# Attention halves turned at the end of their slot, values in the middle of the next; first maximum ahead of the combination; even dense pieces

## Chip, cores and metric

One Trainium2 chip (trn2), one of its cores. The metric is the device time of one execution in microseconds (us), the median of several runs.

## The reference

The kernel computes a two-layer encoder trunk on x (1, 1024, 1024), all in float32. Each layer projects a normed input to queries, keys and values of three groups of attention heads, adds one output projection of their outputs, and then a squared-ReLU MLP. Cut to what matters:

```python
for l in range(DEPTH):                                  # 2
    proj = rmsnorm(x, g_mix[l]) @ w_in[l]
    # A: 4 heads, differential: softmax(q1 k1) - lam * softmax(q2 k2), times v (128 wide), then rmsnorm per head
    # B: 4 heads, window of the last 2 chunks of 64 keys, with a sink logit in maximum and sum
    # C: 4 heads, causal with forget gates: s + cum[q] - cum[k]
    x = x + concat([o_a, o_b, o_c]) @ w_out[l]
    x = x + square(relu(rmsnorm(x, g_mlp[l]) @ w_up[l])) @ w_down[l]
return rmsnorm(x, g_final)
# inside each group, for a block of 128 queries:
s = q @ k.T * scale + bias          # only allowed keys
p = softmax(s)                      # A: a = p[0] - lam * p[1]
o = p @ v
```

## The kernel before

Every float32 product is made of three matmuls of a faster type: each operand is split into a high part (rounded, a copy by ScalarE) and a low part (the rest, a subtraction by VectorE), and high*high, low*high and high*low are summed in PSUM. So everything that TensorE multiplies must first pass through ScalarE and then VectorE.

The part that the change touches is the attention loop, one per layer. Its work is a list of 64 *steps*: eight pairs of heads in the order B0, B1, C0, C1, A0, A1, A2, A3, and in each pair i = 0 to 7, the blocks of 128 queries. A step covers `window(t)` blocks of keys: at most 2 in B, i + 1 in C and A. Scores of up to 512 keys are one *phase*; steps with more than 4 key blocks have two (`phases(t)`), and both use the same PSUM tile ps[0], so that the second scores wait until the first are read.

What a step t goes through:
- TensorE makes the scores (`scores`, L1211).
- VectorE adds the bias, takes the maximum of each row and writes to probs (`biased_max`, L888, once per phase), then the negated maximum (L900 for B, L904 for two phases, L907 else).
- ScalarE takes exponentials in place (`exponentials`, L613; the sink's at L616), j = 0 and 1 for the two score maps of the pair.
- In A pairs VectorE then combines both maps into one (`combine`, L920); in B and C it inverts the sums (`invert_sums`).
- One step later TensorE turns (transposes) the result in *halves* of up to four 128x128 blocks into one of two banks of ps[2] (`turn_half`, L1264); ScalarE takes the high part (`half_high`, L631), VectorE the low part (`half_low`, L943).
- TensorE multiplies a half with V into ps[3] (`values`, L1284 and L1286), VectorE adds up both columns (`sum_values`, L952 and L961), and ScalarE scales the output or squares it for the later norm (`finish_o`, L646 and L639).

A *slot* is the unit of the order written out by hand: each half of step t-1 gets one slot in step t, so a step has one to four slots (A: one half per four key blocks; C: the same for each of two heads). In the slots of steps 56, 57, 58 and 62 halves of finished head outputs are turned too, for the output projection (mix slots, L626 and L938). The engines all run over the same list of slots, each in its own fixed order, and meet through semaphores.

Between these, to fill TensorE, stand *pieces* of the projection for later pairs: a slab of 128 output columns is 8 pieces (one per 128 input rows) of six matmuls of 512 columns (`piece`, L1116), accumulated in ps[1] alone, so the next slab's first piece waits until VectorE has taken the slab out (`evacuate`, L801 for Q and L804 for K and V). Then ScalarE and VectorE split it (`part_high` L576, `part_low` L814, L816); a V slab is turned first (L1097, then L571 and L811). `PIECES` says how many pieces each step of a pair gets. Weights come by DMA into one buffer w_raw, are split by ScalarE (w_hi, L520) and GpSimd (w_lo, L498), from slab 23 on by VectorE (w_lo, L769), and only then is the next load issued on SP's queue. From slab 23 the slabs belong to the output projection (`add_out`, L979); xw_hi (L514) is a further load there.

TensorE's order in a slot before:

```python
early = (len(s.pieces) + 1) // 2
if s.first and t < NT:
    scores(t, 0)
dense(s.pieces[:early])
if s.half: turn_half(s.half)
if s.values: values(s.values)        # the half of the slot before
...                                  # a V slab is turned here
if s.first and t < NT and phases(t) == 2:
    scores(t, 1)
dense(s.pieces[early:])
```

## Time and profile before

| what | us |
|---|---|
| median of 3 runs (2870.1 to 2870.88) | 2870.24 |
| the profiled execution | 2878.04 |
| its span, first to last instruction | 2876.2 |
| TensorE busy (93% of the span) | 2674.1 |
| VectorE busy | 1164.2 |
| ScalarE busy | 897.7 |
| GpSimd busy | 192.8 |
| mean granted TensorE clock | 0.952 of full speed |

The durations come from the one profiled execution. TensorE is busy nearly all of the time, but a busy figure also counts time at a lower granted clock. The kernel has stages with different limits: the attention loops lie at about 87 to 645 us (layer 0) and 1497 to 2058 us (layer 1), with a tail of some 20 us each, and between and behind them come output projection and MLP. A row of the view by windows reads: stretch (us from the span's start), its length, busy us of TensorE's matmuls, its weight loads, VectorE, ScalarE and GpSimd (each with its count), then the mean granted clock of TensorE, the DMA share and GB/s.

### The profile page before, as it was taken

What the parts mean: (1) busy time and instruction counts of PE and PEld (TensorE: products, weight loads), DVE (VectorE), ACT (ScalarE), POOL (GpSimd) and SP (SyncE); (2) the same over time, 40 slices, a digit from 0 to 9 for tenths busy, and PEclk for the clock granted to TensorE, in tenths of its full rate; (3) what the DMA queues carried; (4) which work ended last, traced back from release to release, by engine and by line L of the source; (5) the groups of instructions that cost most, each with busy time, mean ns of one, the idle gap of its engine ahead of it and who ended that gap; (6) DMA issues with size and microseconds to landing.
All of it is one profiled execution on the core that took longest, in us unless ns stands there. A gap on an engine that the chain in (4) does not pass through costs nothing.

```text
span 2876.2 us, 34048 instructions
## 1 busy us (share of the span) xinstructions
PE 2674.1 (93%) x12857; PEld 2175.5 (76%) x12857; DVE 1164.2 (40%) x2367; ACT 897.7 (31%) x1580; POOL 192.8 (7%) x91
## 2 busy tenths in 40 slices
PE   8989988778999999999999989887799999999998
PEld 6777766657888888888877777665688888888886
DVE  5553455555322322223336445555553222232233
ACT  5543333443221212112236343343332112121222
POOL 1010111001000000000210110110020000000001
PEclk9998899988999999999999989997899999999999
DMA  5000000021111111111210000001111111111112
GB/s 165 23 23 15 23 23 23 21 64 47 37 51 51 44 51 46 49 51 51 95 44 23 23 15 23 23 23 53 35 52 44 51 44 51 44 51 51 44 51 73
DMA packets 218717, 127.22 MB, mean 44 GB/s; under 512 B 15182, under 2 KB 214392, under 8 KB 218616
## 3 DMA queue, kind: packets, MB, share of 16 engines
q1 hardware_dynamic: 213192, 114.35, 13.9%
q10 hardware_dynamic: 5424, 11.54, 1.1%
q8 instruction: 62, 1.02, 0.2%
q14 instruction: 39, 0.32, 0.0%
HBM read 113.27 MB, written 12.58 MB: 44 GB/s over the span
## 4 chain that ended last, share of the span: by engine, by line
PE 84%; DVE 7%; ACT 5%; issue 3%; DMA 1%; DVEq 0%; SPq 0%; ACTq 0%; POOL 0%; POOLq 0%
PE ps L1116 72%; PE ps L1264 3%; PE ps L1211 3%; PE ps L1284 2%; ACT probs L613 2%; PE ps L1286 1%; DVE probs L920 1%; ACT pt_hi L631 1%; PE ps L1097 1%; DVE part L804 1%; PE ps L1161 1%; DVE part L801 1%; DVE probs L888 1%; DVE pt_lo L943 1%; DVE wide_lo L938 0%
## 5 line engine op out<-in xcount | busy, mean ns | idle before, releaser
L1116 PE MATMUL ps<-wide_hi,w_hi 128*128 128x512 f32 x3016 | 976.8, 406 | 66.2 <-DVE part L804 31.9
L1116 PE MATMUL ps<-wide_lo,w_hi 128*128 128x512 f32 x3016 | 947.9, 396 | 0.0
L1116 PE MATMUL ps<-wide_hi,w_lo 128*128 128x512 f32 x3016 | 944.8, 395 | 0.0
L1116 PEld LDWEIGHTS ps<-wide_hi,w_hi 128*128 128x128 f32 x3016 | 555.5, 192 | 203.8 <-issue 90.0
L1116 PEld LDWEIGHTS ps<-wide_lo,w_hi 128*128 128x128 f32 x3016 | 578.7, 192 | 125.9
L1116 PEld LDWEIGHTS ps<-wide_hi,w_lo 128*128 128x128 f32 x3016 | 576.1, 191 | 124.3
L631 ACT ACTIVATE pt_hi<-ps 128x512 fp32r<-128x512 f32 (+3 forms) x216 | 110.0, 511 | 482.0 <-PE ps L1264 481.9
L687 ACT ACTIVATE w_hi<-w_raw 128x1024 fp32r<-128x1024 f32 x112 | 117.8, 1051 | 451.8 <-PE ps L1116 450.7
L943 DVE TENSOR_TENSOR pt_lo<-ps,pt_hi 128x512 fp32r<-128x512 f32 (+3 forms) x216 | 126.5, 587 | 301.1 <-ACT pt_hi L631 301.1
L1284 PE MATMUL ps<-v_parts,pt_hi 128*128 128x128 f32 (+1 forms) x696 | 204.5, 353 | 21.9 <-DVE pt_lo L943 21.9
L691 ACT ACTIVATE ring<-ring 128x1024 f32<-128x1024 f32 x64 | 67.8, 1060 | 492.2 <-DVE ring L1051 492.2
L1071 DVE TENSOR_TENSOR xt<-ps,xt 128x1024 f32 x48 | 58.8, 1225 | 387.5 <-PE ps L1116 387.5
L1051 DVE SCALAR_TENSOR_TENSOR ring<-ps,inv_rms 128x1024 f32<-128x1024 f32 x64 | 78.4, 1225 | 331.4 <-PE ps L1116 314.6
L613 ACT ACTIVATE probs<-probs,neg_max,slope 128x256 f32<-128x256 f32 (+7 forms) x256 | 201.3, 788 | 14.2 <-DVE neg_max L904 10.3
L1264 PE MATMUL ps<-ident,probs 128*128 128x128 f32 x696 | 130.0, 305 | 73.0 <-DVE probs L920 73.0
L1264 PEld LDWEIGHTS ps<-ident,probs 128*128 128x128 f32 x696 | 95.1, 157 | 105.2 <-issue 86.6
L1284 PEld LDWEIGHTS ps<-v_parts,pt_hi 128*128 128x128 f32 x696 | 150.5, 216 | 30.0 <-DVE pt_lo L943 27.6
L1286 PE MATMUL ps<-v_parts,pt_lo 128*128 128x64 f32 (+1 forms) x696 | 170.8, 253 | 0.0
L498 POOL TENSOR_TENSOR w_lo<-w_raw,w_hi 128x1024 fp32r<-128x1024 f32 x42 | 104.2, 2481 | 903.2 <-ACT w_hi L520 903.2
L1286 PEld LDWEIGHTS ps<-v_parts,pt_lo 128*128 128x128 f32 x696 | 150.9, 217 | 0.1
L1054 DVE TENSOR_TENSOR wide_lo<-ring,wide_hi 128x1024 f32 x64 | 78.4, 1226 | 158.1 <-ACT wide_hi L693 158.1
L1047 DVE TENSOR_TENSOR w_lo<-w_raw,w_hi 128x1024 fp32r<-128x1024 f32 x112 | 136.4, 1218 | 0.4 <-ACT w_hi L687 0.4
(140 smaller groups left out, 1899.8 us busy)
## 6 DMA issues: line engine op xcount, KB each, us to landing
w_raw<-in_w_up_dram SPq DMA_DIRECT2D x128, 256.0 KB, 3.0
w_raw<-in_w_down_dram SPq DMA_DIRECT2D x128, 256.0 KB, 3.0
w_raw<-in_w_in_dram SPq DMA_DIRECT2D x92, 256.0 KB, 3.3
x_saved<-xt ACTq DMA_DIRECT2D x16, 512.0 KB, 2.6
w_raw<-in_w_out_dram SPq DMA_DIRECT2D x32, 256.0 KB, 3.3
xt<-x_saved SPq DMA_DIRECT2D x16, 512.0 KB, 3.6
out_dram<-rows SPq DMA_DIRECT2D x4, 1024.0 KB, 6.7
first_rows<-in_x_dram ACTq DMA_DIRECT2D x3, 1024.0 KB, 13.3
```

The costliest lines, as they stand in the source:

```text
L498: nc.gpsimd.tensor_tensor(w_lo[:, j], w_raw[:], w_hi[:, j].bitcast(F32), ALU.subtract).then_inc(w_split, 1)
L613: e = A.activation(probs[:, (2 * t + j) % 4, 0:width], probs[:, (2 * t + j) % 4, 0:width], ACT.Exp, bias=neg_max[:, at:at + 1], scale=sl, ...
L631: A.activation(pt_hi[:, bank, 0:half.blocks], src.rearrange("p (b q) -> p b q", q=P), ACT.Copy).then_inc(pt_hi_done, 1)
L687: A.activation(w_hi[:, w_slot(l, FFN_DONE + j)], w_raw[:], ACT.Copy).then_inc(w_hi_done, 1)
L943: V.tensor_tensor(pt_lo[:, bank, 0:half.blocks], src.rearrange("p (b q) -> p b q", q=P), pt_hi[:, bank, 0:half.blocks].bitcast(F32), ALU.s ...
L1047: V.tensor_tensor(w_lo[:, z], w_raw[:], w_hi[:, z].bitcast(F32), ALU.subtract).then_inc(w_split, 1)
L1051: V.scalar_tensor_tensor(out=ring[j][:], in0=ps[j][:], scalar=0.0, in1=inv_rms[:], op0=ALU.max, op1=ALU.mult).then_inc(evacuated, 1)
L1116: mm = T.matmul(ps[p][:, bass.ts(t, BANK)], w, h[:, bass.ts(t, BANK)], start=(start and n == 0), stop=(stop and n == 2))
L1211: mm = T.matmul(ps[0][:, BANK * j:BANK * j + key1 - key0], q[half, q_slot(p), i * P:(i + 1) * P], k[half, kv_slot(p), k0 * P + key0:k0 * P ...
L1264: tr = T.transpose(ps[2][:, at:at + P], src[:, b * P:(b + 1) * P], ident[:])
L1284: T.matmul(o.rearrange("p (h e) -> p h e", h=2), pt_hi[:, bank, at], v_parts[:, kv_slot(p), k0 + b, :, e], start=(b == 0), stop=False)
L1286: mm = T.matmul(o[:, 0:w], pt_lo[:, bank, at], v_parts[:, kv_slot(p), k0 + b, 0, e], start=False, stop=(b == blocks - 1))
```

## The change

On TensorE, the half of a slot is turned at the slot's end, and the values of the slot before stand behind its early pieces, ahead of the second scores; the turn of a V slab moves up to just behind the first scores. On VectorE, the first maximum of a step comes ahead of the combination (or inversion) of the step before, and the low part of a half behind the evacuation. On ScalarE, a slot's exponentials come ahead of its high part, the first exponentials of a two-phase step in its first slot instead of its second; `finish_o` comes one slot later. The maximum of the second phase starts from that of the first, so that one negation serves both. `PIECES` is more even, and of a slot's pieces at least two, or all but one, count as early. From pair 2 on the first slot of i = 0 gets no piece.

```diff
--- before.py
+++ after.py
@@ -37,6 +37,7 @@
         self.pieces, self.ends, self.ended, self.split = [], None, None, []
         self.turns_v = None
         self.summed = None
+        self.stored = None
         self.exps = []
 
 
@@ -119,9 +120,9 @@
     PHASE0 = [sum(phases(u) for u in range(t)) for t in range(NT + 1)]
     NPHASE = PHASE0[NT]
 
-    PIECES = {0: [2] * 8, 1: [2] * 8, 2: [0, 3, 4, 4, 4, 4, 3, 2], 3: [0, 3, 4, 4, 4, 4, 3, 2]}
+    PIECES = {0: [2] * 8, 1: [2] * 8, 2: [0, 3, 3, 3, 3, 4, 4, 4], 3: [3, 3, 3, 3, 3, 3, 3, 3]}
     for p in range(FIRST_A, PAIRS - 1):
-        PIECES[p] = [0, 4, 4, 4, 3, 3, 3, 3]
+        PIECES[p] = [2, 3, 3, 3, 3, 3, 3, 4]
     PIECES[PAIRS - 1] = [0, 1, 3, 4, 4, 3, 3, 0]
     MIX_AT = {56: [0, 1], 57: [2, 3], 58: [4, 5], 62: [6]}
     SCALE_AT = {FIRST_A * NQ + 2 * NQ + 3: (0, 2), FIRST_A * NQ + 3 * NQ + 3: (2, 3)}
@@ -174,6 +175,8 @@
             now = [s for s in mine if s.step % NQ == i]
             want = PIECES[p][i] + held
             for k, s in enumerate(now):
+                if i == 0 and k == 0 and p >= 2:
+                    continue
                 n = -(-want // (len(now) - k))
                 for _ in range(n):
                     if not todo:
@@ -192,6 +195,7 @@
         s.values = last.half if last and last.half and last.half.slab is None else None
         if s.values and s.values.last:
             s.summed = s.values.step
+        s.stored = last.summed if last else None
         done = slots[n - 1].ends if n else None
         if done is not None and (done >= IN or SLABS[done][1] != V_):
             s.ended = done
@@ -207,7 +211,7 @@
     for t in range(NT):
         now = [s for s in slots if s.step == t]
         for j in range(2):
-            at = 0 if phases(t) == 1 else 1 + j
+            at = 0 if phases(t) == 1 else j
             now[min(at, len(now) - 1)].exps.append(j)
 
     def load_done(n):
@@ -651,19 +655,21 @@
                     A.activation(o_inv[:, n0 * NQ:n1 * NQ], o_inv[:, n0 * NQ:n1 * NQ], ACT.Sqrt).then_inc(o_rms, 1)
 
                 for s in slots:
-                    if s.half:
-                        half_high(s.half)
                     if s.ended is not None and s.ended < IN:
                         part_high(s.ended)
                     for j in s.exps:
                         exponentials(s.step, j)
-                    if s.summed is not None:
-                        finish_o(s.summed)
+                    if s.stored is not None:
+                        finish_o(s.stored)
+                    if s.half:
+                        half_high(s.half)
                     for n in s.split:
                         split_load(l, n)
                     if s.step in SCALE_AT and s.first:
                         rms_of_heads(*SCALE_AT[s.step])
 
+                if slots[-1].summed is not None:
+                    finish_o(slots[-1].summed)
                 finish_o(NT - 1)
                 rms_of_heads(3, 4)
                 split_load(l, EXTRA + 1)
@@ -876,6 +882,8 @@
                     if before:
                         dve.wait_ge(turned, NHALF * l + before[-1])
                     V.memset(wait_slot[:], 0.0)
+                    if ph:
+                        dve.wait_ge(scores_read, NPHASE * l + PHASE0[t] + 1)
                     to = far_max if ph else row_max
                     a = (2 * t) % 8
                     for j in range(2):
@@ -887,8 +895,8 @@
                             bias = o_out[:, FIRST_A + 2 * n + j, key0:key1]
                         e = V.tensor_tensor_reduce(out=probs[:, (2 * t + j) % 4, key0:key1],
                                                    in0=ps[0][:, BANK * j:BANK * j + key1 - key0], in1=bias, scale=1.0,
-                                                   scalar=-3e38, op0=ALU.add, op1=ALU.max,
-                                                   accum_out=to[:, a + j:a + j + 1])
+                                                   scalar=row_max[:, a + j:a + j + 1] if ph else -3e38,
+                                                   op0=ALU.add, op1=ALU.max, accum_out=to[:, a + j:a + j + 1])
                     e.then_inc(scores_read, 1)
                     if key1 < width:
                         return
@@ -899,12 +907,8 @@
                             at = 4 * l + 2 * p + j
                             e = V.tensor_scalar(neg_max[:, a + j:a + j + 1], row_max[:, a + j:a + j + 1], sink[:, at:at + 1],
                                                 neg_slope[:, 2 * p + j:2 * p + j + 1], ALU.max, ALU.mult)
-                    elif ph:
-                        for j in range(2):
-                            e = V.tensor_scalar(neg_max[:, a + j:a + j + 1], row_max[:, a + j:a + j + 1],
-                                                far_max[:, a + j:a + j + 1], neg, ALU.max, ALU.mult)
                     else:
-                        e = V.tensor_scalar(neg_max[:, a:a + 2], row_max[:, a:a + 2], neg, None, ALU.mult)
+                        e = V.tensor_scalar(neg_max[:, a:a + 2], to[:, a:a + 2], neg, None, ALU.mult)
                     e.then_inc(max_done, 1)
 
                 def combine(t):
@@ -982,19 +986,15 @@
                 dve.wait_ge(cum_out, CH * (l + 1))
                 for s in slots:
                     t = s.step
+                    if s.first and t < NT:
+                        biased_max(t, 0)
                     if s.first and t:
                         if ORDER[(t - 1) // NQ][0] == "A":
                             combine(t - 1)
-                    if s.first and t < NT:
-                        biased_max(t, 0)
-                    if s.half:
-                        half_low(s.half)
+                        else:
+                            invert_sums(t - 1)
                     if s.first and t < NT and phases(t) == 2:
                         biased_max(t, 1)
-                    if s.first and t and ORDER[(t - 1) // NQ][0] != "A":
-                        invert_sums(t - 1)
-                    if s.summed is not None:
-                        sum_values(s.summed)
                     if s.ended is not None and s.ended < IN:
                         part_low(s.ended)
                     if s.ends is not None:
@@ -1002,6 +1002,10 @@
                             evacuate(s.ends)
                         else:
                             add_out(s.ends - OUT)
+                    if s.half:
+                        half_low(s.half)
+                    if s.summed is not None:
+                        sum_values(s.summed)
                     for n in s.split:
                         if n >= IN:
                             split_load(l, n)
@@ -1290,20 +1294,20 @@
 
                 for s in slots:
                     t = s.step
-                    early = (len(s.pieces) + 1) // 2
+                    early = max(min(2, len(s.pieces)), len(s.pieces) - 1)
                     if s.first and t < NT:
                         scores(t, 0)
-                    dense(s.pieces[:early])
-                    if s.half:
-                        turn_half(s.half)
-                    if s.values:
-                        values(s.values)
                     if s.turns_v is not None:
                         pe.wait_ge(evacuated, EVACS * l + slab_of(s.turns_v, V_) + 1)
                         turn(part, ps[1], NQ, v_turned)
+                    dense(s.pieces[:early])
+                    if s.values:
+                        values(s.values)
                     if s.first and t < NT and phases(t) == 2:
                         scores(t, 1)
                     dense(s.pieces[early:])
+                    if s.half:
+                        turn_half(s.half)
 
                 def out_piece(k, slab, p, start, stop):
                     j = w_slot(l, OUT + k)
```

## Rows read from the trace of the kernel before

**Rows 1.** The page, its 40 slices: TensorE busy in tenths.
```profile
PE   8989988778999999999999989887799999999998
```

**Rows 2.** TensorE's waits over the span: us in total, times, longest us.
```profile
PE ps L1264 <- DVE probs L920: 73.0, 36, 5.9
...
PE ps L1116 <- DVE part L804: 31.9, 12, 3.0
...
PE ps L1284 <- DVE pt_lo L943: 21.9, 21, 2.9
```

**Rows 3.** Windows: B, C0, C1, A0, A1, A2, A3 of layer 1; A1 of layer 0.
```profile
1496.80:1575.60 78.80, 76.03 (x450) 59.91 (x450) 46.83 (x177) 49.09 (x144) 7.16 (x3) 0.97 0.08 22
1575.60:1658.70 83.10, 74.26 (x425) 60.15 (x424) 37.05 (x114) 33.84 (x77) 7.25 (x3) 0.91 0.07 20
1658.70:1748.30 89.60, 80.73 (x457) 66.79 (x456) 38.52 (x116) 33.68 (x77) 7.23 (x3) 0.89 0.07 18
1748.30:1822.00 73.70, 65.61 (x358) 51.91 (x356) 40.55 (x122) 26.98 (x66) 7.61 (x3) 0.93 0.08 22
1822.00:1895.10 73.10, 63.19 (x334) 49.87 (x332) 41.55 (x123) 28.03 (x67) 7.68 (x3) 0.91 0.09 23
1895.10:1972.90 77.80, 64.21 (x336) 49.83 (x334) 44.71 (x127) 30.85 (x70) 8.55 (x4) 0.91 0.08 21
1972.90:2076.00 103.10, 74.37 (x375) 59.17 (x375) 59.07 (x149) 42.71 (x90) 1.90 (x1) 0.81 0.19 55
413.70:484.00 70.30, 59.81 (x336) 46.53 (x334) 41.67 (x123) 28.10 (x67) 7.65 (x3) 0.98 0.09 23
```

**Rows 4.** VectorE's groups by shape: busy us, mean ns of one, idle before.
```profile
L943 DVE TENSOR_TENSOR pt_lo<-ps,pt_hi 128x512 fp32r<-128x512 f32 x128 | 88.2, 691 | 152.9 <-ACT pt_hi L631 152.8
...
L804 DVE TENSOR_TENSOR part<-ps,inv_rms 128x1024 f32<-128x1024 f32 x28 | 34.1, 1218 | 21.3 <-PE ps L1116 21.1
...
L904 DVE TENSOR_SCALAR neg_max<-row_max,far_max,neg_slope 128x1 f32<-128x1 f32 x96 | 21.8, 269 | 5.3 <-issue 0.9
...
L888 DVE CUSTOM_DVE_ANT_0 probs<-ps,near 128x256 f32<-128x256 f32 x56 | 21.4, 420 | 14.6 <-issue 14.6
...
L888 DVE CUSTOM_DVE_ANT_0 probs<-ps,far 128x384 f32<-128x384 f32 x32 | 16.5, 553 | 10.6 <-issue 10.6
...
L907 DVE TENSOR_SCALAR neg_max<-row_max,neg_slope 128x2 f32<-128x2 f32 x48 | 12.5, 260 | 5.0 <-issue 0.4
...
L920 DVE SCALAR_TENSOR_TENSOR probs<-probs,lam_ratio 128x1024 f32<-128x1024 f32 x8 | 10.3, 1285 | 0.6
```

**Rows 5.** TensorE's timeline in layer 0, pair A1 and A2's start.
```profile
456.27 0.30 PE L1264 MATMUL ps<-ident,probs 128*128 128x128 f32 x1 [0.79 <-DVE probs L920]
...
461.30 0.47 PE L1116 MATMUL ps<-wide_hi,w_hi 128*128 128x512 f32 x1 [2.98 <-DVE part L804]
...
462.76 0.27 PE L1264 MATMUL ps<-ident,probs 128*128 128x128 f32 x1
...
469.97 0.73 PE L1116 MATMUL ps<-wide_hi,w_hi 128*128 128x512 f32 x2
...
472.83 0.38 PE L1264 MATMUL ps<-ident,probs 128*128 128x128 f32 x2
...
488.19 0.45 PE L1264 MATMUL ps<-ident,probs 128*128 128x128 f32 x1 [3.67 <-DVE probs L920]
```

**Rows 6.** ScalarE's groups by shape, columns as in the groups above.
```profile
L631 ACT ACTIVATE pt_hi<-ps 128x512 fp32r<-128x512 f32 x128 | 75.7, 594 | 260.2 <-PE ps L1264 260.2
...
L613 ACT ACTIVATE probs<-probs,neg_max,slope 128x256 f32<-128x256 f32 x80 | 47.2, 591 | 1.4 <-DVE neg_max L907 1.2 <-DVE neg_max L900 0.2
...
L646 ACT ACTIVATE o_out<-o_out,inv_sum 128x64 f32<-128x64 f32 x128 | 37.1, 338 | 48.5 <-DVE o_out L961 48.5
...
L613 ACT ACTIVATE probs<-probs,neg_max,slope 128x896 f32<-128x896 f32 x24 | 27.0, 1126 | 0.0
...
L616 ACT ACTIVATE sink_exp<-sink,neg_max,slope 128x1 f32<-128x1 f32 x64 | 23.9, 374 | 0.0
```

## The prediction

> **What bounds the kernel now.** I read the page first. TensorE's tenths show where it is slack: slices 2 to 9 and 21 to 29 [rows 1]. These are the two attention loops (one per layer), and everything that the diff touches lies in them. Next, TensorE's waits [rows 2]: longest for the combination (L920), then for a projection slab to be taken out of PSUM (L804, and L801 for Q slabs), then for low parts (L943). Then the loop of layer 1 pair by pair [rows 3]. Stretch less TensorE's busy time is its idle time: B pairs 2.8, C0 8.8, C1 8.9, A0 8.1, A1 9.9, A2 13.6, A3 with the tail 28.7 us, in all 81 us a layer. VectorE and ScalarE are busy at most 62% of any stretch, so it is the order of the work that costs time, not its amount.
>
> The half-rate clock is the second loss. Pair A1 took 70.3 us in layer 0 at a mean clock of 0.98 and 73.1 us in layer 1 at 0.91 [rows 3]. The 0.07 are 10 us more at 1.2 GHz instead of 2.4, and they cost 2.8 us: 0.28 us for each us at half rate. Over the 579 us from B to A3 the mean clock is about 0.91, so some 105 us at half rate, 29 us lost a layer.
>
> **The change, part by part.** No engine gets work worth counting, and no DMA is added; SP's loads wait for w_split as before. Removed: in the 24 two-phase steps of a layer (i = 4 to 7 of the C and A pairs) two L904 instructions become one of L907's form, 269+269 to 260 ns [rows 4]: 0.25 us off a dependent chain. Added: row_max as scalar operand of the second maximum, and a wait on VectorE's own first maximum. No row shows the operand; nearest is L904, which reads such a column and takes 9 ns more than L907, which reads none. From below nothing, from above 0.1 us a step (the wait on itself with it), 5 us in all; I take 0, as the first maximum ended long before.
>
> Moved at no price of its own: finish_o a slot later (nobody waits for it before the mix slots), the turn of V to behind the first scores (what then waits is in the terms "V slab" below), and the same 24 pieces a pair spread more evenly, where they fall being part of each walk.
>
> *Combination and turn later.* Before, in step i=5 of A1, TensorE does scores and one piece and then waits 0.79 us at the turn for the combination; the slab that ended there costs 2.98 us more; in step i=0 it has no piece at all and waits 3.7 us [rows 5]. Now the turn stands at the slot's end, behind its pieces, values and second scores.
>
> *What comes in its place.* ScalarE's order in a slot is now exponentials, then high part. In the first slot of a two-phase step the exponentials need the second maximum, and this the second scores, which TensorE issues just ahead of the turn. So the high part of that half is queued behind second maximum, negation and first exponentials; after it comes the low part; and TensorE wants both after one piece of the next slot. For A, i=6, from the end of the second scores: 0.05 + two maxima of 384 (0.55+0.48) + 0.1 + negation 0.23 + 0.03 + exponentials of 896 1.03 (1126 ns, less the 0.1 by which neighbours overlap) + high part 0.59 + 0.03 + low part 0.69 + 0.14 = 3.9 us [rows 4, 6]. Cover: turn 0.38 and one piece 1.46 (461.30 to the next engine work at 462.76) [rows 5], 1.84. Wait: 2.1 us. In the same way i=7 of A (two pieces cover) 1.2; and C, i = 4, 5, 6, 7: 1.35, 1.7, 2.1, 2.5, together 7.65 a pair.
>
> *Slots without a piece.* There values follow directly on their own turn: high 0.59 + low 0.69 + hops 0.2 = 1.5 us uncovered [rows 4, 6]. The plan leaves such slots last in C1's i = 5, 6, 7 and in A0's i=0: four times 1.5 a layer. Before, the transposes of the next half stood between.
>
> *Pair by pair, TensorE's idle us a layer* (before from [rows 3]):
> - C0: V slab at i=1 0.5, slab at i=3 0.3, and 7.65: 8.45; before 8.8: **-0.4**.
> - C1: V slab at i=0 1.4, slab at i=5 0.2, 7.65, three bare slots 4.5: 13.75; before 8.9: **+4.9**.
> - A0: V slab 1.4, bare slot 1.5, i=5 2.65, i=6 2.1, i=7 1.2: 8.85; before 8.1: **+0.8**. The i=5, from its start: VectorE begins the first maximum at 2.85, behind the low part of i=4, ends it at 4.2 and the combination at 5.65; TensorE is ready for the turn at 5.15 and, with the hop, waits 0.65. The second maximum ends at 6.85, the slab's evacuation (1.22) [rows 4] at 8.1; its next piece was wanted at 6.2: 2.0.
> - A1: i=0 2.85, i=3 0.2, then as A0: 9.0; before 9.9: **-0.9**. The i=0: low part of i=7's last half at 1.1, first maximum to 2.0, combination of 1024 (1.29 and two small ones) [rows 4] to 3.9; TensorE is ready at 2.0; then the V slab's low part ends 0.85 later than the turn.
> - A2: the same, and 1.4 for the w_lo that VectorE makes itself in i=5: 10.4; before 13.6: **-3.2**.
> - A3: walked the same way. The first piece of slab 25 waits 2.85 for w_lo (before 1.6), since VectorE comes to it after the half of i=3, whose high part is behind both exponentials. The second exponentials of i=5 still stand behind xw_hi, which waits for its DMA: this was the longest wait, 5.9 [rows 2], and is now spread over a low part (4.0), second scores (1.1) and the turn (0.9). Second scores ahead of the turn in i=7 give time back. From slab 24 to the tail +0.4, mix slots of i = 0, 1 -0.4: **0**.
>
> *Fewer switches.* Two pieces in one run take 2.86 us (469.97 to 472.83), one alone 1.46 [rows 5] and up to 0.1 more after scores: 0.06 to 0.2 saved where two runs become one. Four merges in each of three A pairs, at 0.13: **-1.5**.
>
> *B pairs.* The slab waits go (-2.8), and 16 merges at 0.2, since both runs there follow another kind of work, take 3.2: a full step of 4.67 us, from 4.88. But VectorE and ScalarE now form a ring: maxima and negation 1.33 (two of 0.42, two of 0.27, less overlap), exponentials with sinks 1.82 (0.59 and 0.37, twice, overlapped), scaling of the outputs 0.5 (0.34 twice, overlapped), high part 0.6, low part 0.65, value sum 0.25: 5.15 us [rows 4, 6]. That is longer than the step. The slack is used up after five steps or so; ten more cost 0.48 each and two short ones give 1 back: +3.8. B: **-2.2**.
>
> Sum a layer: -2.2 -0.4 +4.9 +0.8 -0.9 -3.2 +0 -1.5 = -2.5; two layers -5.
>
> *The clock.* The long waits shrink: before, some twelve of 2.8 us or more a layer; now about three, but fifteen of 2.0 to 2.6. Half rate follows such waits: the transpose behind 3.67 us takes 0.45 us where the one behind 0.79 takes 0.30 [rows 5]. Bounds: nothing comes back, or all of 29 us a layer. I take 2 a layer, near nothing, since as many waits remain as go: -4. The Trainium skill (TensorE: Matmul & The Clock Gate, "HAM oscillation") says that waits between bursts of matmuls throttle the engine when they are long, and that short ones leave it at full rate. By that rule alone the sum would be that of rival 2.
>
> Total -9: the profiled execution's 2878.04 us would be 2869. It lies 7.8 above the median of the timed runs, 2870.24, so the median becomes **2861**. A tie is anything within 0.2% (5.7 us), about what a measurement of this kernel can tell from no change.
>
> **Rivals.**
> 1. *The ring of VectorE and ScalarE decides: slower.* For A, i=7, it is first maximum 1.5, combination 1.9, second maximum and negation 1.7, exponentials 1.3, high part 0.6, exponentials 1.4, high and low part and sum 1.7: 10.1 us, as long as TensorE's step of four pieces (9.7). If lag carried over makes each of the 48 two-phase steps 0.5 us longer than I sum, it is +24: 2885. It decides from 0.2 us each. For it: no reserve in i = 5 to 7. Against: VectorE is busy only 57% of A1 [rows 3].
> 2. *The clock recovers.* Waits of 2.6 us keep full rate; of the 58 us two thirds come back, less a third of that for the waits that stay: -26 where I take -4: 2838. For it: 10 us less at half rate were worth 2.8 in A1. Against: waits of 2 to 3 us every ten.
> 3. *The late turn hides nearly everything.* The waits for L920 (73.0) go and nothing replaces them: about 2800. Against: the order on ScalarE above.
> 4. *No net effect.* One wait for another, 2870.
>
> **How the numbers follow.** Forecast (own range 2850 to 2871) 0.36, of it 0.26 beyond the tie and 0.10 in it; rival 1 0.32 (0.28 slower, 0.04 tie); rival 2 0.14; rival 3 0.06; rival 4 0.12 (0.08 tie, 0.04 slower). Faster 0.46, same 0.22, slower 0.32. The range, 2828 to 2893, holds the forecast, rivals 2 and 4 and most of rival 1, with the 5 us of the unpriced operand; it leaves out rival 3.
>
> **What would show it.** Waits for L920 and for the slabs fall to a third or less; those for L943 grow from 21.9 to 80 or more, some 2 us each, at i = 4 to 7 of C and A; the B stretch is 76 to 77 us, C1 longer than 92; busy times of VectorE and ScalarE stay. I am wrong if the low-part waits stay small (then rival 3), if B steps stay at 4.7, or if steps i = 5 to 7 of the A pairs exceed 12 us (rival 1).

## The result, and the profile after

The changed kernel takes **2885.65 us** (median of 4 runs, 2882.95 to 2887.71), the one before 2870.17 beside it: ratio 1.0056, 95% interval 1.0038 to 1.0073. So it is 15 us slower, where the forecast was 9 us faster. The number lies in the range given, and the sign was wrong. Its profiled execution took 2882.95 us (span 2881.1, mean clock 0.954), that of before 2878.04. The two profiles alone show only a third of the loss, so a second one of each kernel was taken; what follows uses both.

TensorE's waits of the kernel after (us in total, times, longest us); they answer to [rows 2]. L947 is the low part (L943 before), L924 the combination (L920), L810 the evacuation of K and V slabs (L804):
```profile
PE ps L1288 <- DVE pt_lo L947: 88.1, 54, 3.2
PE ps L1268 <- DVE probs L924: 17.5, 22, 1.7
PE ps L1120 <- DVE part L810: 16.9, 10, 2.3
```
The combination went from 73.0 to 17.5, slabs from 31.9 to 16.9, and low parts from 21.9 to 88.1, 1.6 us each. This is the exchange that the prediction describes.

Windows of layer 1 (B, C0, C1, A0, A1, A2, A3 with the tail; length, PE busy, ... granted clock as third from the end), as in [rows 3]:
```profile
1498.50:1575.50 77.00, 75.28 (x450) 61.48 (x450) 45.11 (x174) 46.28 (x135) 7.12 (x3) 0.98 0.10 28
1575.50:1659.60 84.10, 73.93 (x423) 58.40 (x422) 39.20 (x114) 35.79 (x83) 7.17 (x3) 0.94 0.07 20
1659.60:1756.30 96.70, 82.70 (x459) 66.45 (x458) 37.77 (x112) 35.11 (x76) 7.10 (x3) 0.89 0.07 17
1756.30:1833.10 76.80, 69.45 (x359) 54.61 (x358) 43.00 (x118) 29.77 (x68) 7.16 (x3) 0.88 0.08 21
1833.10:1900.50 67.40, 59.82 (x333) 46.45 (x332) 41.17 (x118) 28.11 (x66) 7.20 (x3) 0.97 0.09 24
1900.50:1973.40 72.90, 62.93 (x335) 48.90 (x334) 44.06 (x123) 31.00 (x69) 9.11 (x4) 0.93 0.08 23
1973.40:2080.45 107.05, 78.42 (x375) 59.63 (x375) 55.79 (x143) 40.48 (x86) 1.90 (x1) 0.76 0.18 53
```
Length less busy time is idle time. In C1 it is 14.0 us (13.75 forecast, 8.9 before), in A2 10.0 (10.4 forecast, 13.6 before). In A3 with the tail it is 28.6, as before (28.7), but TensorE's busy time there rose from 74.4 to 78.4 us at a clock of 0.76 instead of 0.81 [rows 3]. So the case is decided by busy time too, and not by the waits alone.

The same stretch, C1, in three places: layer 0 of the first profile of the changed kernel,
```profile
250.60:345.00 94.40, 80.40 (x457) 64.67 (x456) 37.84 (x112) 35.01 (x76) 7.10 (x3) 0.91 0.07 18
```
and layers 0 and 1 of its second profile:
```profile
255.80:356.40 100.60, 86.61 (x457) 69.53 (x456) 37.77 (x112) 35.10 (x76) 7.10 (x3) 0.84 0.06 16
...
1672.70:1767.20 94.50, 80.51 (x459) 64.76 (x458) 37.85 (x112) 34.98 (x76) 7.09 (x3) 0.91 0.06 17
```
The idle time is 14.0 us in all three. What varies is how much of the work runs at 1.2 GHz. From 0.91 of 94.4 us to 0.84 of 100.6 us are 15 us more at half rate (twice 0.16 of 100.6, less twice 0.09 of 94.4), and they cost 6.2: 0.41 us each, not the 0.28 that the prediction took.

Over both loops with their tails, from the first scores to the first piece behind the last step, the sums are:

| | idle us | busy us |
|---|---|---|
| before, two profiles | 160.9, 160.1 | 994.8, 992.6 |
| after, two profiles | 164.8, 164.8 | 1001.6, 1010.8 |
| difference of the means | +4.3 | +12.5 |

Together 16.8 us, of which the rest of the program gives 4.6 back in these four executions; the loss is 15.5 us here and, by its ratio, some 21 in the repeat below.

The 12.5 us of busy time have two parts. One is the clock: over both loops and tails (twice the length of a window times what its clock lacks of 1) TensorE was granted 1.2 GHz for 225 and 225 us before, and for 226 and 250 after. At 0.41 us each these 13 us more are some 5, an estimate. The other part is there at an unchanged clock. The first profile of the changed kernel has as much time at half rate as the kernel before, and yet 7 to 9 us more busy time. The loop of layer 1, before and after:
```profile
1496.80:2057.54 560.74, 487.77 (x2672) 388.77 (x2673) 296.37 (x899) 237.97 (x570) 47.37 (x20) 0.91 0.09 26
...
1498.49:2059.15 560.66, 491.11 (x2671) 387.10 (x2672) 295.88 (x876) 240.69 (x571) 46.75 (x20) 0.91 0.10 27
```
The executions say the same: at a mean clock of 0.953 the kernel before took 2866.9 to 2872.3 us (11 executions), the changed one 2884.9 to 2887.7 (3). So of the 16.8 us some 4 are waiting, 5 the lower clock, and 7 busy time that the new order costs at the same clock. That half rate fell on dearer work does not explain them: with each matmul put at the mean that it has at the full clock between the same neighbours, over all profiles here, the loops come to 903 and 902 us before and 910 and 911 after (high_first of experiment 1: 906, hf_bare of experiment 7: 903), an estimate. No run isolates these 7. What the traces show is that TensorE is interrupted more often: in the loops it idled for longer than 0.15 us 102 and 98 times before, and 126 and 125 times after (100 in high_first, 88 in hf_bare). And a run is dearer at its start: in the timeline at the end of this section the first matmul of the values takes 0.39 us behind its wait, the next of its kind (478.06) 0.33.

How one late low part comes about, in the timeline of layer 0, pair A1, step i=6, second slot (start, duration, in brackets the wait before):
```profile
473.68 0.63 PE L1268 MATMUL ps<-ident,probs 128*128 128x128 f32 x4
...
475.02 0.23 DVE L911 TENSOR_SCALAR neg_max<-far_max,neg_slope 128x2 f32<-128x2 f32 x1
475.29 1.14 ACT L617 ACTIVATE probs<-probs,neg_max,slope 128x896 f32<-128x896 f32 x1 [5.04 <-DVE neg_max L911]
...
476.42 0.57 ACT L635 ACTIVATE pt_hi<-ps 128x512 fp32r<-128x512 f32 x1
...
477.03 0.69 DVE L947 TENSOR_TENSOR pt_lo<-ps,pt_hi 128x512 fp32r<-128x512 f32 x1 [1.78 <-ACT pt_hi L635]
...
477.77 0.39 PE L1288 MATMUL ps<-v_parts,pt_hi 128*128 128x256 f32 x1 [2.08 <-DVE pt_lo L947]
```
The half is turned by 474.31. ScalarE had been idle for 5 us, but in its order the exponentials come first, and they wait for the negation; the high part starts 2.1 us after it could have. The values wait 2.08 us; the prediction says 2.1.

### The profile page after: what moved, and what is told of

Its sections match the earlier page's. It is cut to its first block, busy times and chain, and to the rows that moved or that the text cites. A ratio compares the mean times of both kernels' runs of the same rounds, so it can differ in the third digit from the quotient of the medians.

```text
span 2881.1 us, 34000 instructions
## 1 busy us (share of the span) xinstructions
PE 2675.7 (93%) x12857; PEld 2168.9 (75%) x12857; DVE 1161.7 (40%) x2319; ACT 901.9 (31%) x1580; POOL 191.6 (7%) x91
## 3 DMA queue, kind: packets, MB, share of 16 engines
q8 instruction: 62, 1.02, 0.1%
## 4 chain that ended last, share of the span: by engine, by line
PE 73%; issue 10%; DVE 9%; ACT 6%; DVEq 2%; DMA 0%; SPq 0%; ACTq 0%; POOL 0%; POOLq 0%
PE ps L1120 64%; PE ps L1288 3%; DVE probs L896 2%; PE ps L1268 2%; ACT pt_hi L635 2%; DVE pt_lo L947 1%; ACT probs L617 1%; PE ps L1290 1%; PE ps L1215 1%; DVEq L903 1%; DVE neg_max L911 1%; PE ps L1165 1%; DVEq L920 1%; ACT wide_hi L630 1%; DVE probs L924 0%
## 5 line engine op out<-in xcount | busy, mean ns | idle before, releaser
L1120 PE MATMUL ps<-wide_hi,w_hi 128*128 128x512 f32 x3016 | 977.4, 406 | 44.1 <-DVE part L810 16.9
L947 DVE TENSOR_TENSOR pt_lo<-ps,pt_hi 128x512 fp32r<-128x512 f32 (+3 forms) x216 | 127.0, 588 | 378.9 <-ACT pt_hi L635 378.7
L1288 PE MATMUL ps<-v_parts,pt_hi 128*128 128x128 f32 (+1 forms) x696 | 186.7, 328 | 88.6 <-DVE pt_lo L947 88.1
L1288 PEld LDWEIGHTS ps<-v_parts,pt_hi 128*128 128x128 f32 x696 | 144.6, 208 | 122.9 <-DVE pt_lo L947 116.4
L1055 DVE SCALAR_TENSOR_TENSOR ring<-ps,inv_rms 128x1024 f32<-128x1024 f32 x64 | 78.4, 1225 | 329.9 <-PE ps L1120 313.1
L1268 PE MATMUL ps<-ident,probs 128*128 128x128 f32 x696 | 131.0, 305 | 17.7 <-DVE probs L924 17.5
L1058 DVE TENSOR_TENSOR wide_lo<-ring,wide_hi 128x1024 f32 x64 | 78.4, 1226 | 158.1 <-ACT wide_hi L699 158.1
L1268 PEld LDWEIGHTS ps<-ident,probs 128*128 128x128 f32 x696 | 82.6, 151 | 32.7 <-issue 28.5
```

The source lines that it names most:

```text
L947: V.tensor_tensor(pt_lo[:, bank, 0:half.blocks], src.rearrange("p (b q) -> p b q", q=P), pt_hi[:, bank, 0:half.blocks].bitcast(F32), ALU.s ...
L1055: V.scalar_tensor_tensor(out=ring[j][:], in0=ps[j][:], scalar=0.0, in1=inv_rms[:], op0=ALU.max, op1=ALU.mult).then_inc(evacuated, 1)
L1058: V.tensor_tensor(u_lo[:, 2 * m + j], ring[j][:], u_hi[:, 2 * m + j].bitcast(F32), ALU.subtract).then_inc(u_split, 1)
L1120: mm = T.matmul(ps[p][:, bass.ts(t, BANK)], w, h[:, bass.ts(t, BANK)], start=(start and n == 0), stop=(stop and n == 2))
L1268: tr = T.transpose(ps[2][:, at:at + P], src[:, b * P:(b + 1) * P], ident[:])
L1288: T.matmul(o.rearrange("p (h e) -> p h e", h=2), pt_hi[:, bank, at], v_parts[:, kv_slot(p), k0 + b, :, e], start=(b == 0), stop=False)
```

## The experiments

**Repeats.** Each kernel unchanged, for a second profile (above) and a second ratio.

> The kernel before, unchanged, for a second profile. Theory A (the loss lies in the order of the engines) expects 2867 to 2873 us, idle time of TensorE from B to the start of step 63 again 73 us a layer, and time at half rate within 25 us of the first profile. Theory B (the half-rate clock differs from execution to execution enough to make the difference) expects a profiled time that differs by 8 us or more from the first profile's 2878, with the idle time unchanged.

Measured: 2868.09, ratio 0.9996 (0.9977 to 1.0015).

> The changed kernel, unchanged, for a second profile and a second ratio. Theory, the loss is real and the same each time: ratio 1.004 to 1.007, 2880 to 2890. Rival, most of the 15 us was the scatter of executions: ratio 1.000 to 1.003.

Measured: 2893.9, ratio 1.0072 (1.0044 to 1.0100), just above what was expected. The loss is real.

**1. The high part ahead of the exponentials.** ScalarE's order in a slot becomes slab's high part, half's high part, exponentials. finish_o, which now runs closer to its successor on the scratch tile o_junk, gets a wait for its own last squaring:
```diff
+                    if s.half:
+                        half_high(s.half)
                     for j in s.exps:
                         exponentials(s.step, j)
                     if s.stored is not None:
                         finish_o(s.stored)
-                    if s.half:
-                        half_high(s.half)
```


> The changed kernel, but ScalarE takes a half's high part ahead of the exponentials of the same slot (with a wait of each squaring in the A pairs on the one before, since both write the same scratch tile). Theory A (the high part queued behind the exponentials costs about 2 us in each of 48 two-phase steps) expects the waits for low parts to fall from 88 to 30 us or less and the time to 2820 to 2845 us. The rival (VectorE's and ScalarE's chain through the step sets its length, in whatever order) expects the waits to move to the combination and the time to stay within 2875 to 2890.

Measured: **2807.45**, ratio 0.9797 (0.9764 to 0.9831), 78 us faster than the change and 63 faster than before. The same slot as above:
```profile
444.66 0.63 PE L1270 MATMUL ps<-ident,probs 128*128 128x128 f32 x4 [1.24 <-DVE probs L926]
...
445.33 0.60 ACT L635 ACTIVATE pt_hi<-ps 128x512 fp32r<-128x512 f32 x1 [4.08 <-PE ps L1270]
...
445.96 0.69 DVE L949 TENSOR_TENSOR pt_lo<-ps,pt_hi 128x512 fp32r<-128x512 f32 x1
...
446.70 0.39 PE L1290 MATMUL ps<-v_parts,pt_hi 128*128 128x256 f32 x1
```
The high part starts 0.04 us after the turn's end, and the values don't wait; the turn itself waits 1.24 us for the combination (see the last section). Waits for low parts fall to 41.7 us in all, not to the 30 that was expected. Pair C0 in both layers:
```profile
161.50:234.10 72.60, 68.92 (x423) 54.87 (x422) 38.23 (x112) 35.63 (x83) 7.16 (x3) 1.00 0.09 23
...
1533.20:1605.80 72.60, 68.93 (x426) 54.89 (x424) 38.25 (x112) 35.62 (x83) 7.15 (x3) 1.00 0.09 23
```
Idle 3.7 instead of 10.2, busy 68.9 instead of 73.9 to 78.5, at the full 2.4 GHz. Over both loops idle time falls by 40.9 us (to 123.9) and busy time by 41.9 (1006.2 to 964.3): for each us of waiting that went, another of busy time went too. Most of it is clock, with 154 us at half rate in the loops instead of 226 and 250. That is why the gain is beyond what was expected.

**2. Where does the clock come back?** The same edit in the slots of the C pairs only, and everywhere else only:
```diff
+                    early_high = s.half and 2 <= s.step // NQ < FIRST_A
+                    if early_high:
+                        half_high(s.half)
```


> The changed kernel with the high part of a half ahead of the exponentials only in the slots of the two C pairs; elsewhere as in the change. In high_first TensorE's idle time in the C pairs fell from 24.2 to 12.7 us a layer and its busy time there by some 10 us a layer, which is the clock. Theory, idle time and clock go together in the stretch where the wait is, whatever stands elsewhere: 23 us of idle and 15 to 25 of clock come back, 2838 to 2852, and the mean clock of the two C0 stretches is 1.00. Rival, the clock of a stretch follows the whole load, not its own waits: 2855 to 2866, with C0 still at 0.9 to 0.95.

> The complement: the high part first everywhere but in the C pairs. The B pairs' idle time (4.2 and 1.7 us in B1) and that of A0 to A2 (25 to 19 a layer) come back, some 18 us in all, and as much of clock in them. Theory: 2845 to 2860, the C0 stretches stay at 0.88 to 0.94 and C1 at 0.84 to 0.91. Rival, as above: the C stretches' clock rises too and the time is under 2840.

Measured: 2853.29, ratio 0.9941 (0.9925 to 0.9958), and 2849.25, ratio 0.9928 (0.9900 to 0.9956). Pairs C0 and A1 of layer 1 with the C pairs alone,
```profile
1567.10:1640.70 73.60, 69.39 (x424) 54.95 (x424) 37.35 (x115) 35.73 (x83) 7.16 (x3) 1.00 0.09 22
...
1807.80:1875.20 67.40, 59.84 (x335) 46.44 (x334) 41.16 (x118) 28.10 (x66) 7.20 (x3) 0.97 0.09 24
```
and with all but them:
```profile
1562.80:1646.00 83.20, 73.58 (x425) 58.41 (x424) 38.02 (x112) 35.67 (x83) 7.18 (x3) 0.94 0.07 20
...
1815.90:1879.60 63.70, 57.94 (x335) 45.63 (x334) 41.99 (x119) 27.79 (x66) 7.50 (x3) 1.00 0.10 26
```
C0's clock rises with C0's own waits gone, A1's with A1's. The gains over the change are 32.4 and 36.4 us, in sum 68.8 of high_first's 78.2. The theory's place was right, its price for C a little high: idle fell by 25.0 us as expected, busy time by 11 instead of 15 to 25: C1 still has 8.7 us of idle time, and its clock stays at 0.88 to 0.91. The rival, a clock that follows the whole load alone, is out. But a stretch's own waits are not all either: C0 was expected at 1.00 in both layers, and in layer 0 it is 0.96, with the same 4.2 us of idle time as in layer 1. There B1 just ahead of it still has 4.1 us of waits, which high_first, with 1.00 in both, has not.

**3. The rest of ScalarE's new order.** High part first, ahead of the slab's high part too, and the exponentials of two-phase steps a slot later, as before the change:
```diff
-        at = 0 if phases(t) == 1 else j
+        at = 0 if phases(t) == 1 else 1 + j
...
+                    if s.half:
+                        half_high(s.half)
                     if s.ended is not None and s.ended < IN:
                         part_high(s.ended)
...
-                    if s.half:
-                        half_high(s.half)
```


> The changed kernel with ScalarE's order of before in each slot (high part of the half first, then the slab's high part, then exponentials, these one slot later in two-phase steps), finish_o a slot later as in the change. Theory, the change lost its gain by queuing the high part behind the exponentials: 2805 to 2840, waits of the values for the low part below 50 us (88 in the changed kernel). With the exponentials a slot later the combination is later too, so nearer 2830 than high_first's 2807. Rival, the ring of VectorE and ScalarE is too long whatever the order: 2870 to 2890.

Measured: 2876.49, ratio 1.0028 (1.0013 to 1.0043): missed. Low parts fell to 49.6 us as said, but other waits are longer than in high_first (there 28.3, 8.9 and 8.2 for the last three lines in turn):
```profile
PE ps L1290 <- DVE pt_lo L949: 49.6, 38, 3.5
PE ps L1270 <- DVE probs L926: 40.4, 30, 2.9
PE ps L1122 <- DVE v_parts L819: 27.7, 10, 3.0
PE ps L1217 <- DVE row_max L898: 16.7, 13, 3.2
```
From high_first this kernel differs by 69 us, and in two things: the late exponentials, and the half's high part ahead of the slab's. Of the 47.2 us of idle time between them (171.1 and 123.9 in the loops) 18.8 are waits for v_parts. These belong to the second: ScalarE copies a V slab only when it is through with the high part of a half that TensorE turned late. The combination and the first maximum (12.1 and 8.5) fit the late exponentials. So early exponentials look like the good part of the change on ScalarE, and the high part behind them is the bad one (experiment 1); how the 69 us divide was not measured.

This kernel also warns of a simple rule for the clock: it idles 6.3 us more than the change and is busy 26 us less, with some 205 us at half rate.

**4. Single parts of the change on the old kernel.** TensorE's new order alone (with the earlier turn of a V slab and the new count of early pieces, not shown here), and the first maximum ahead of the combination alone:
```diff
-                    if s.half:
-                        turn_half(s.half)
                     if s.values:
                         values(s.values)
...
                     dense(s.pieces[early:])
+                    if s.half:
+                        turn_half(s.half)
```


> The kernel before with only TensorE's order changed: V slab turned behind the first scores, pieces, values, second scores, then the turn at the slot's end. VectorE, ScalarE and the pieces as before. Theory A expects a gain, as high parts are not behind exponentials: waits for the combination from 73 to 35 us or less, for low parts at most 35, 2840 to 2860 us. The rival (a turn late in the slot is itself the loss, since the low part comes late for the values) expects 2875 us or more and waits for low parts above 60 us.

```diff
+                    if s.first and t < NT:
+                        biased_max(t, 0)
                     if s.first and t:
                         if ORDER[(t - 1) // NQ][0] == "A":
                             combine(t - 1)
-                    if s.first and t < NT:
-                        biased_max(t, 0)
```


> The kernel before with only VectorE's order changed: first maximum ahead of the combination. The turn stays in mid slot, so each combination comes 1.4 us later for it. Theory A expects waits for the combination to grow by 1.0 to 1.4 us in 30 to 48 steps, from 73 to 105 to 140 us, and 2900 to 2930 us. A rival (the maximum first frees the exponentials earlier and pays for itself) expects 2870 or less.

Measured: 3070.67, ratio 1.0708 (1.0674 to 1.0743), and 2899.45, ratio 1.0127 (1.0088 to 1.0166). The second came just under what was expected, with 96.5 us of waits for the combination instead of 105 or more. Its idle time in the loops is 23 us above the kernel before, its busy time the same (992.3; before 994.8 and 992.6). The first was missed by 200 us; the rival had the right side, with low parts at 74.7 us and above 2875, but not the size. These waits come with it:
```profile
PE ps L1211 <- DVE row_max L888: 66.7, 29, 5.2
PE ps L1116 <- DVE part L804: 47.9, 12, 4.3
PE ps L1116 <- DVE part L801: 32.4, 14, 2.8
```
VectorE's old order has the low part ahead of the second maximum and of the evacuation. With the turn at the slot's end that low part comes late, and both are queued behind it. The change's TensorE order thus needs its VectorE order; neither part can be priced on the old kernel by itself. (The second kernel of experiment 7 puts the low part alone back ahead of the evacuation, and loses 83 us.)

**5. The pieces.** The change with the old counts:
```diff
-    PIECES = {0: [2] * 8, 1: [2] * 8, 2: [0, 3, 3, 3, 3, 4, 4, 4], 3: [3, 3, 3, 3, 3, 3, 3, 3]}
+    PIECES = {0: [2] * 8, 1: [2] * 8, 2: [0, 3, 4, 4, 4, 4, 3, 2], 3: [0, 3, 4, 4, 4, 4, 3, 2]}
     for p in range(FIRST_A, PAIRS - 1):
-        PIECES[p] = [2, 3, 3, 3, 3, 3, 3, 4]
+        PIECES[p] = [0, 4, 4, 4, 3, 3, 3, 3]
```


> The changed kernel with the piece counts of before (none in step i=0 of C and A pairs). Theory, a slot without a piece leaves a half's values right behind its own turn, 1.5 us uncovered: C1 loses its three such slots, but all slots of i=0 of seven pairs a layer become bare, so 2890 to 2915. Rival, the placing of the pieces doesn't matter because the same work is spread either way: 2880 to 2890. If it is under 2875, the even pieces were a loss by themselves.

Measured: 2954.58, ratio 1.0301 (1.0279 to 1.0322), 69 us more, beyond the expected. Low-part waits go from 54 (88.1 us) to 70 (116.5 us), 28 us, and the span's clock from 0.954 to 0.931. TensorE's idle time over the span rises by 21 us, its busy time by 51 (2675.7 to 2727.0). A slot without a piece is about as dear as expected in waiting, and more than twice that again in busy time.

**6. The maxima.** The change without the operand row_max and its wait, with two negations:
```diff
-                                                   scalar=row_max[:, a + j:a + j + 1] if ph else -3e38,
+                                                   scalar=-3e38,
...
```


> The changed kernel with the maxima of before: second maximum without the operand row_max and its wait, two L904-like negations in place of one. Theory, the shorter chain is worth something: second maximum 0.06 us shorter twice, negations 0.25 longer, so the chain is 0.13 us longer in each of the 48 two-phase steps, 2884 to 2892. Rival, the operand and the added wait on the own semaphore cost more than the negation saves: 2870 to 2882.

Measured: 2889.82, ratio 1.0067 (1.0043 to 1.0091), not to be told from the change's 1.0056 and 1.0072. It is inconclusive on the time. The instruction itself is plain in the groups by shape of the changed kernel:
```profile
L896 DVE CUSTOM_DVE_ANT_0 probs<-ps,far 128x512 f32<-128x512 f32 x80 | 51.9, 686 | 5.5 <-issue 5.5
...
L896 DVE CUSTOM_DVE_ANT_0 probs<-ps,far,row_max 128x512 f32<-128x512 f32 x16 | 11.4, 747 | 10.3 <-issue 10.1
```
The operand costs 61 ns at 512 columns (60 at 384), twice a step: half of the 0.25 us that the single negation saves.

**7. Toward a better version.** high_first, and in a slot without a piece the next turn ahead of the last values (and not at the slot's end again):
```diff
+                    if s.half and not s.pieces:
+                        turn_half(s.half)
                     if s.values:
                         values(s.values)
```


> high_first (2807) with one more edit: in a slot without a piece the turn of the next half is issued ahead of the values of the last one. Theory, in such slots (three in C1, one in A0, some in the B pairs' and the tail's steps) values wait 1.5 us for their own turn, and the tail's +3.1 us a layer comes from this: 2790 to 2801, with the stretch from the scores of step 63 to the first piece behind the last turn back to 33 us or less from 35.8. Rival, the wait only moves (the turn now waits in the same place for the combination or the exponentials): 2803 to 2812.

Measured: **2788.62**, ratio 0.9727 (0.9701 to 0.9753): the fastest kernel here, 97 us below the change. Idle 117.1, busy 958.5. The reason that I gave for the tail was wrong: from the scores of step 63 to the next piece it takes 18.4 and 19.2 us, but high_first already took 18.8 and 19.1, where the change takes 21.3. The gain lies in A0 (73.1 and 72.9 us to 68.9 and 67.9; of it in the first step 15.0 and 15.9 to 13.6) and in A3 (85.2 and 84.5 to 82.8 and 82.0). On top of it, the combination ahead of the first maximum again, and the low part ahead of the evacuation:

> hf_bare (2789) with the combination ahead of the first maximum again, as in the kernel before. It tests that part of the change with the late turn in place. Theory, the first maximum must stand first, since the second scores wait for it and the late turn gives the combination cover: without it the 36 combinations of 1.9 us stand ahead of it, and 0.5 to 1 us of each shows: 2810 to 2830. Rival, the combination is now the last one waited for (39 us at the turn), so giving it precedence pays: 2770 to 2785.

> hf_bare (2789) with the low part of a half ahead of the evacuation of the slab that ends in the same slot, on VectorE. Waits for low parts are 30 us, for evacuations 15. Theory, with the high part early on ScalarE the low part can go as soon as it is there, and slots in which a slab ends lose their wait of 1.2 us: 2778 to 2787. Rival, the low part waits for the high one (4.9 at the longest) and holds the evacuation up behind it, as in the kernel before with the late turn: 2795 to 2830.

Measured: 2808.10, ratio 0.9777 (0.9753 to 0.9801), just under its range, and 2871.93, ratio 1.0009 (0.9994 to 1.0024), above both. So the first maximum ahead of the combination is worth 14 us (by the ratios) to 19 (by the medians) with the late turn, where it costs 1.3% without it (experiment 4). In the second, slabs are waited for again,
```profile
PE ps L1270 <- DVE probs L926: 36.7, 24, 5.3
PE ps L1122 <- DVE part L812: 27.5, 12, 2.7
PE ps L1290 <- DVE pt_lo L949: 27.5, 22, 4.4
PE ps L1122 <- DVE part L809: 24.4, 14, 2.5
PE ps L1103 <- DVE part L812: 19.9, 12, 1.8
```
and the low parts gained 2.6 us (30.1 to 27.5). What waits at the head of VectorE's queue, here a low part whose high part is not there yet, holds what stands behind it.

## Why the prediction was wrong

**The waits were right in sum, in part by luck.** TensorE's idle us a layer, forecast and measured (before: layer 1):

| pair | before | forecast | layer 0 | layer 1 |
|---|---|---|---|---|
| B | 2.8 | 3.8 | 4.2 | 1.7 |
| C0 | 8.8 | 8.45 | 10.1 | 10.2 |
| C1 | 8.9 | 13.75 | 14.0 | 14.0 |
| A0 | 8.1 | 8.85 | 7.8 | 7.4 |
| A1 | 9.9 | 9.0 | 7.6 | 7.6 |
| A2 | 13.6 | 10.4 | 10.0 | 10.0 |
| A3 and tail | 28.7 | 28.7 | 31.7 | 28.6 |

The forecast's idle sum is 83.0 a layer, the measured mean 82.4. (B's forecast is its 2.8, less the slab waits, with the ring's 3.8; its switches are busy time.) C0 missed 1.6 us: its step i=0 has no piece either, a bare slot that my list of four left out, and it measures 1.62 at the price of 1.5 that the list used. A0 and A1 were 1 to 1.5 us too dark, because i=5 measures 1.9 instead of 2.65 and, in A1, i=0 2.15 instead of 2.85. A3 with the tail is 3.0 longer in layer 0, which no step of the walk has. The misses of single pairs, up to 3 us, cancel; the single waits that the theory named (C's 1.5, 1.8, 2.2 and 2.6, and 2.08 in A) are no luck.

**TensorE's busy time was wrong.** It was to fall by 13.4 us (9.4 by *Fewer switches* and the merges of *B pairs*, 4 by *The clock*); it rose by 12.5. Both terms failed, and neither had a case with a loss in it.

*The clock*: long waits go, short ones come, so 4 us come back. Instead some 13 us more were at half rate, about 5 us. Three faults are in it.
- It took half rate to follow the longest waits. In C0 the change idles 1.5, 1.8, 2.2 and 2.6 us in steps i=4 to 7, and the clock is 0.92 and 0.94 (0.88 and 0.92 in the second profile); before it was 0.95 and 0.91, with up to 3.1 us in one step. In high_first 1.5 us are the most in any step of C0, and it is 1.00. Waits of about 2 us thus cost the clock no less than the long ones did.
- It bounded the clock from one side: "nothing comes back" was taken as the worst, so no case of the sum had a loss in it. Yet the change had more waits, if shorter ones.
- It priced half rate at 0.28 us a us, by the length of A1; by busy time the same two rows give 3.4 us for 10, or 0.33, and C1 shows 0.41.

The Trainium skill (TensorE: Matmul & The Clock Gate, "A second HAM failure mode: psum-queue depth-cycling") describes a kernel in which frequent short idle times between groups of matmuls make the clock swing between its levels. C0's 0.88 to 0.94 with 10.2 us of short waits, and 1.00 with 3.7 us of them in high_first, agree with it; the section just ahead of it, which the prediction names beside rival 2, speaks of long waits only, and by it alone the clock should have risen.

*Fewer switches* was mis-sized by more. At an unchanged clock busy time was to fall by 9.4 us and rose by about 7. A full B step was to fall from 4.88 to 4.67 us; it takes 4.82 to 4.84. At a full clock 16 merges give 0.04 each and not 0.2, so some 5 us of the 9.4 were not there. The rest lies in the other pairs, where the sum has twelve merges a layer in the A pairs saving 0.13 each, and nothing for the runs that the new, shorter waits cut. That the cutting is what costs the 7 us is likely from the counts above (some 25 interruptions more, and fewer again in the faster kernels), but not shown.

**The rivals.** Rival 1 gave 2885, which is the number measured, but not for its reason, so that the range held the result is luck: of the steps that were priced one by one, in C0 to A2, none idles 0.5 us longer than forecast, so there is no lag that adds up; B1 alone shows some in layer 0 (4.2 us). Steps i=5 to 7 of the A pairs do pass 12 us now and then, which I had named as its mark. A step of A1, i=7, with 1.08 and 1.10 us of idle took 12.02 and 12.62 us, and in high_first 9.69 with none: the mark was the clock's. Rival 2, a clock that recovers, is seen in another kernel: with most waits for low parts gone, 42 us of busy time come back, most of it clock. Rival 3's 2800 needed exactly what experiments 1 and 7 did.

**What would show it** was met by the waits for low parts and combination (88.1, 1.6 us each, and 17.5), by the B stretch of layer 1 (77.0; layer 0 took 80.0), by C1 above 92 and by the unchanged busy times of VectorE and ScalarE. It was not met by the slabs: their waits fell to a half (K, V and Q together 47.2 to 21.6), not to a third.

What stays open: what exactly the 7 us at an unchanged clock are, why the same stretch gets 0.91 in one execution and 0.84 in another with the same waits, and where in a step the clock falls.

## What to carry to other kernels

When an instruction is moved earlier in an in-order queue, list what now stands behind it and whether it waits for a later event: here the place of one call on ScalarE was the difference between 15 us lost and 63 won. When a transfer of waits is even, busy time decides it, so give it a case with a loss. Where the high part was moved, each us of waiting removed took 0.4 to 1 us of busy time with it (25.0 and 11, 19.9 and 18.7, 40.9 and 41.9 us). That is no law: old_scalar idles 6 us more than the change and is busy 26 less, and before_max_first idles 23 more than the kernel before and is busy as long. Parts of a reordering that only work together can't be priced one at a time on the old kernel, but can be undone one at a time on the new.

## What the runs showed of the hardware

A VectorE instruction of 0.228 us took 2.29 when it was issued beside one of GpSimd. Pair A0's first step, in the changed kernel:
```profile
346.63 2.36 POOL L502 TENSOR_TENSOR w_lo<-w_raw,w_hi 128x1024 fp32r<-128x1024 f32 x1 [38.12 <-ACT w_hi L524]
...
346.72 2.29 DVE L911 TENSOR_SCALAR neg_max<-row_max,neg_slope 128x2 f32<-128x2 f32 x1
```
It ends 0.02 us after GpSimd's. In the first C0 step that has pieces the same negation takes 1.58 us (173.60 to 175.18), to the end of a GpSimd split (172.78 to 175.16). Not every instruction is held: in the same stretch the maximum of 256 columns, which reads its scores from PSUM, takes its usual 0.42 us (173.07). The Trainium skill (SBUF — State Buffer, "SBUF: two separate sides") says that VectorE, in an instruction of a two-port mode or with two inputs in SBUF, shares a pair of ports with GpSimd, and that whichever starts first has the pair until it ends; these rows agree. The combination is held too. That of 768 columns takes 1.02 us on average before, and in high_first, where half of the eight run beside a split, 2.04:
```profile
L920 DVE SCALAR_TENSOR_TENSOR probs<-probs,lam_ratio 128x768 f32<-128x768 f32 x8 | 8.1, 1019 | 0.6
...
L926 DVE SCALAR_TENSOR_TENSOR probs<-probs,lam_ratio 128x768 f32<-128x768 f32 x8 | 16.3, 2038 | 0.6
```
In the slot shown in experiment 1 it takes 3.08 us (441.44 to 444.52, the split 441.32 to 443.70), and this is what the turn there waits for. The prediction did not ask which GpSimd splits its moved instructions would meet.
